# Recurrence of a hybrid layer: 32-blocks of the inverse paired into one block-diagonal product, and the value weights split inside the last turn

## The reference, cut to what matters

```python
def _rwkv7_scan(r, w, k, v, a, b):
    def step(state, inp):
        r_t, w_t, k_t, v_t, a_t, b_t = inp
        sa = jnp.einsum('bhvk,bhk->bhv', state, a_t)
        state = (state * w_t[:, :, None, :] + sa[..., None] * b_t[:, :, None, :]
                 + v_t[..., None] * k_t[:, :, None, :])
        return state, jnp.einsum('bhvk,bhk->bhv', state, r_t)
```

## Time and profile before

| what | value |
|---|---|
| median of three runs | 1833.14 us |
| the profiled execution, its time | 1833.6 us |
| its span, first to last instruction | 1831.8 us |
| stretch of the 8 turns of the recurrence | 223.2 to 503.8 us |
| TensorE busy in the whole span | 93% |
| TensorE busy in that stretch | 233 of 280.5 us |
| mean granted clock of TensorE, whole span and stretch | 0.96 and 0.87 of full |

### The profile page before, as it was taken

The page is one execution under the profiler, slowest core; times in us unless marked ns, Lnnn a source line. Parts: engine busy times, 40 slices in busy tenths (PEclk is TensorE's granted clock), DMA queues, the critical chain, the costliest instruction groups (busy, mean ns, idle before and its releaser), DMA issues. The chain is left out here.

```text
span 1831.8 us, 35801 instructions
## 1 busy us (share of the span) xinstructions
PE 1696.0 (93%) x15658; PEld 888.1 (48%) x15658; DVE 788.4 (43%) x1044; ACT 560.0 (31%) x873; POOL 454.4 (25%) x236
## 2 busy tenths in 40 slices
PE   5999678888889999889999999899999999999997
PEld 2444366766644455544444444444444444444443
DVE  5766555567422455611310168632323232332328
ACT  5212253455322455631221226431203021221210
POOL 1221122112021111212333302362325141423220
PEclk9999787899889999999999999999999999999999
DMA  9463000000102020041212031222111120202002
GB/s 356 145 195 126 12 4 4 4 4 4 50 24 70 24 58 1 1 138 35 57 46 57 0 115 35 92 93 69 35 59 47 49 84 19 81 24 92 0 1 92
DMA packets 105700, 109.94 MB, mean 60 GB/s; under 512 B 2508, under 2 KB 82522, under 8 KB 105306
## 3 DMA queue, kind: packets, MB, share of 16 engines
q1 hardware_dynamic: 105560, 107.82, 18.3%
HBM read 101.52 MB, written 4.19 MB: 58 GB/s over the span
## 5 line engine op out<-in xcount | busy, mean ns | idle before, releaser
L208 PE MATMUL tokens_ps<-a_hi,z 128*128 128x512 bf16 x960 | 248.9, 381 | 2.9 <-ACT ff_r L2167 2.8
L591 PE MATMUL ff_ps<-ff_hi,c_hi 128*128 128x512 bf16 x512 | 194.0, 379 | 0.9 <-DVE z L2271 0.9
L591 PE MATMUL ff_ps<-ff_lo,c_hi 128*128 128x512 bf16 x512 | 194.0, 379 | 0.0
L591 PE MATMUL ff_ps<-ff_hi,c_lo 128*128 128x512 bf16 x512 | 194.0, 379 | 0.0
L2271 DVE TENSOR_TENSOR z<-ff_ps,z 128x512 f32<-128x512 f32 x128 | 88.3, 690 | 204.6 <-PE ff_ps L591 204.2
L2167 ACT ACTIVATE ff_r<-tokens_ps,cols 128x1024 f32<-128x1024 f32 x32 | 35.6, 1114 | 436.6 <-PE tokens_ps L208 427.4
L208 PEld LDWEIGHTS tokens_ps<-a_hi,z 128*128 128x128 bf16 x960 | 94.0, 98 | 117.3 <-issue 5.3
L2094 POOL TENSOR_TENSOR z<-z 128x1024 bf16<-128x1024 f32 x28 | 62.2, 2221 | 352.8 <-ACT z L2090 352.8
L208 PE MATMUL tokens_ps<-a_lo,z 128*128 128x512 bf16 x480 | 143.2, 380 | 0.0
L2259 DVE TENSOR_TENSOR ff_r<-ff_r 128x1024 f32<-128x1024 f32 x32 | 41.1, 1285 | 226.9 <-ACT ff_r L2167 226.7
L185 POOL TENSOR_TENSOR mg_wlo<-mg_stage,mg_whi 128x1024 bf16<-128x1024 f32 x21 | 45.7, 2177 | 158.0 <-ACT mg_whi L181 158.0
(11 more groups left out here) (352 smaller groups left out, 3162.9 us busy)
## 6 DMA issues: line engine op xcount, KB each, us to landing
ada_w<-w_ada SPq DMA_DIRECT2D x8, 2048.0 KB, 8.1
ff_st<-w_ff SPq DMA_DIRECT2D x8, 2048.0 KB, 7.8
z<-w_ff SPq DMA_DIRECT2D x30, 512.0 KB, 4.1
mg_stage<-w_in SPq DMA_DIRECT2D x16, 512.0 KB, 4.1
zs_stage<-w_in SPq DMA_DIRECT2D x14, 512.0 KB, 6.9
z<-w_ada SPq DMA_DIRECT2D x6, 1024.0 KB, 13.5
z<-w_in SPq DMA_DIRECT2D x8, 512.0 KB, 4.9
z<-w_out SPq DMA_DIRECT2D x1, 4096.0 KB, 14.3
```

The source lines that it names most:

```text
L208: last = pe.matmul(out[:, h * HALF:(h + 1) * HALF], w[:, kt, :], a[:, slot, h * HALF:(h + 1) * HALF], start=(x == 0 and y == 0), stop=(x = ...
L591: last = pe.matmul(out, a[:, slot, at], w[:, x, n], start=(x == 0 and y == 0), stop=(x == k - 1 and y == 2))
```

## The change

Four edits in the recurrence:

1. The two 32-blocks of a chunk become one 64x64 block-diagonal matrix. `X` and `NTm` become 64 wide (masks of the levels with zeros outside the two diagonal blocks), and `correction` and `corrected` loop over 2 row groups of 64 instead of 4 of 32: 16 products, with 64x64 weights and 32 moving columns.
2. `X` must be block-diagonal, so ScalarE's copy becomes two copies, each scaled by a column of zeros and ones (`misc(5)`, `misc(6)`), each on half of the columns.
3. The roles of `Ts` and `TTs` are exchanged: the sum goes to `TTs` (semaphore `TTe`) and the transpose to `Ts` (semaphore `Te`, four more counts), because `X` is now the weights of `corrected`. The `correction` of the next step waits for `Te`.
4. The 8 `value_weight` of the last turn are no longer behind the scaling of `PQ` but spread over the turn: behind `vn`, correction 2, `kn`, correction 3, `centred`, `T12e`, `squared` and `answers`. `rhs` now shares the buffer of `PQ`, with a wait for `HY` of the turn before ahead of `an`.

The constants `misc` move into the free columns of `small`, and the tile `levels` becomes two. GpSimd's list and SyncE's are unchanged.

The diff, cut to its core (left out: the other uses of `misc` and unchanged lines):

```diff
...
@@ -55,18 +56,20 @@
     t[:, CT["small"]] = np.select([which == 0, which == 1], [upper(1), row == col], 0)
-    t[:, CT["levels"]] = np.select([which == k for k in range(4)], [upper(2 << k) for k in range(4)])
+    own = i % CH // 32 == j % CH // 32
+    for k in range(4):
+        t[:, CT["levels"] + k // 2] += np.where(own & (j // CH == k % 2), upper(2 << k), 0)
     t[:, CT["bones"]] = i // HD == j // HD
...
@@ -896,14 +899,15 @@
                   for at in (PAIRS, PAIRS + 2)] for c in (g.c_hi, g.c_lo))
-        NTd, NTm = sb("NTd", (P, NB, CH)), sb("NTm", (P, NB, 3, B))
-        X, TTs, Ts, T64 = sb("X", (P, NB, B)), sb("TT", (P, NB, B)), sb("T", (P, NB, B)), sb("T64", (P, NB, CH))
-        rhs, PQ = sb("rhs", (P, NB, P)), sb("PQ", (P, NB, P))
+        NTd, NTm = sb("NTd", (P, NB, CH)), sb("NTm", (P, NB, 3, CH))
+        X, TTs, Ts, T64 = sb("X", (P, NB, CH)), sb("TT", (P, NB, B)), sb("T", (P, NB, B)), sb("T64", (P, NB, CH))
+        PQ = sb("PQ", (P, NB, P))
+        rhs = PQ
         gt, st = sb("gt", (P, NC, HD)), sb("st", (P, NC + 1, HD))
...
         BAB, BCD, HY = (BA, BB), (BC, BD), (HY0, HY1)
-        per_turn = {"M1e": 2, "NTd": 2, "NTm": 2, "PQa": NT, "M2e": 2, "TTm": 2, "T12e": 2, "ze": 2, "ge": 2, "ysb": 2, "PQ": 2, "TTe": 4, "Te": 5, "X": 4, "Xe": 4, "TX": 4,
+        per_turn = {"M1e": 2, "NTd": 2, "NTm": 2, "PQa": NT, "M2e": 2, "TTm": 2, "T12e": 2, "ze": 2, "ge": 2, "ysb": 2, "PQ": 2, "TTe": 4, "Te": 5, "X": 4, "Xe": 8, "TX": 4,
                     "ch": NC, "S": NC}
@@ -1021,7 +1025,9 @@
                 wait(act, t, "X", k + 1)
-                act.activation(flat(X[:]), BD[:, 0:2 * P], ACT.Copy).then_inc(s["Xe"], 1)
+                for h in range(2):
+                    act.activation(X[:, :, h * B:(h + 1) * B], BD[:, 0:2 * P].rearrange("p (b n) -> p b n", n=B), ACT.Copy,
+                                   scale=g.misc(5 + h)).then_inc(s["Xe"], 1)
 
@@ -1072,10 +1078,17 @@
                     act.wait_ge(s["vw"], 16)
+                    wait(act, TURNS - 1, "k2")
                 act.activation(v_hi[:, kt, :], v_stage[:, kt, :], ACT.Copy).then_inc(s["vhi"], 1)
...
                 f, n, l, ll, lll = t % 2, t + 1, t - 1, t - 2, t - 3
+
+                def values_ahead(*kts):
+                    if t == TURNS - 1:
+                        for kt in kts:
+                            value_weight(kt)
+
                 state_maps(l)
@@ -1084,30 +1097,36 @@
                 natural(t, "vn", flat(vn[:]), BA[:])
+                values_ahead(0)
                 correction(t, 2)
+                values_ahead(1)
                 decays(n)
                 natural(t, "kn", flat(kn[:]), BB[:])
+                values_ahead(2)
                 correction(t, 3)
+                values_ahead(3)
                 natural(t, "bn", W[f][:, :, 1, :].rearrange("p (e j) n -> p j e n", e=2), q4(BA).rearrange("p j (e n) -> p j e n", e=2))
+                wait(act, l, "HY")
                 natural(t, "an", rhs[:, :, 0:HD].rearrange("p (e j) n -> p j e n", e=2), q4(BB).rearrange("p j (e n) -> p j e n", e=2))
...
                 centred(ll)
+                values_ahead(4)
                 wait(act, t, "T12")
...
                 act.activation(T64[0:B, :, B:CH], BC[0:B, 0:2 * P].rearrange("p (b n) -> p b n", n=B), ACT.Copy).then_inc(s["T12e"], 1)
+                values_ahead(5)
                 wait(act, t, "mv")
...
                 squared(ll)
+                values_ahead(6)
                 high(lll)
                 answers(l)
+                values_ahead(7)
                 wait(act, t, "PQ", 2)
...
                     act.activation(PQ[:, 4 + j, :], BB[:, j * P:(j + 1) * P], ACT.Copy, scale=rn[t % 2][:, 2 * j + 1:2 * j + 2]).then_inc(s["PQa"], 1)
-                if t == TURNS - 1:
-                    for kt in range(KT):
-                        value_weight(kt)
 
@@ -1151,8 +1170,8 @@
             eye = small(1)
-            level = lambda k: g.tile("levels")[:, k * B:(k + 1) * B]
-            upper_levels = g.tile("levels")[:, B:4 * B].rearrange("p (k n) -> p k n", n=B).unsqueeze(1).to_broadcast([P, NB, 3, B])
+            levels = g.const[:, CT["levels"]:CT["levels"] + 2, :].rearrange("p a (k n) -> p (a k) n", n=CH)
+            upper_levels = levels[:, 1:4, :].unsqueeze(1).to_broadcast([P, NB, 3, CH])
             strict, incl = (g.tile("causal")[:, x * CH:(x + 1) * CH] for x in range(2))
@@ -1283,10 +1302,11 @@
                 wait(dve, t, "TX", k + 1)
-                wait(dve, t, "Te", k + 1)
-                dve.tensor_tensor(flat(Ts[:]), BD[:, 2 * P:4 * P], flat(Ts[:]), ALU.add).then_inc(s["Te"], 1)
-                wait(dve, t, "Te", k + 2)
-                dve.transpose(flat(TTs[:]), flat(Ts[:])).then_inc(s["TTe"], 1)
+                if k:
+                    wait(dve, t, "TTe", k)
+                dve.tensor_tensor(flat(TTs[:]), BD[:, 2 * P:4 * P], flat(TTs[:]), ALU.add).then_inc(s["TTe"], 1)
+                wait(dve, t, "TTe", k + 1)
+                dve.transpose(flat(Ts[:]), flat(TTs[:])).then_inc(s["Te"], 1)
 
@@ -1306,9 +1326,9 @@
                 dve.transpose(flat(Ts[:]), flat(TTs[:])).then_inc(s["Te"], 1)
-                dve.tensor_tensor(X[:], NTd[:, :, 0:B], over(level(0), NB), ALU.mult).then_inc(s["NTm"], 1)
+                dve.tensor_tensor(X[:], NTd[:], over(levels[:, 0, :], NB), ALU.mult).then_inc(s["NTm"], 1)
                 queries(l, 1)
-                dve.tensor_tensor(NTm[:], NTd[:, :, 0:B].unsqueeze(2).to_broadcast([P, NB, 3, B]), upper_levels, ALU.mult).then_inc(s["NTm"], 1)
+                dve.tensor_tensor(NTm[:], NTd[:].unsqueeze(2).to_broadcast([P, NB, 3, CH]), upper_levels, ALU.mult).then_inc(s["NTm"], 1)
                 queries(l, 0)
@@ -1338,7 +1358,7 @@
                 wait(dve, t, "X21")
-                dve.tensor_copy(flat(X[:]), BD[:, 0:2 * P]).then_inc(s["X21e"], 1)
+                dve.tensor_copy(X[:, :, 0:B], BD[:, 0:2 * P].rearrange("p (b n) -> p b n", n=B)).then_inc(s["X21e"], 1)
                 state(l, 7)
...
@@ -1536,17 +1556,17 @@
                 for e, j, b in blocks:
-                    for q in quads:
-                        last = pe.matmul(BD[q, b * B:(b + 1) * B], NTm[q, b, k - 1, :] if k else X[q, b, :], Ts[q, b, :], start=True, stop=True)
+                    for rows in rows2:
+                        last = pe.matmul(BD[rows, b * B:(b + 1) * B], NTm[rows, b, k - 1, :] if k else X[rows, b, :], Ts[rows, b, :], start=True, stop=True)
                 last.then_inc(s["X"], 1)
...
             def corrected(t, k):
-                wait(pe, t, "Xe", k + 1)
+                wait(pe, t, "Xe", 2 * k + 2)
                 if k:
...
                 for e, j, b in blocks:
-                    for q in quads:
-                        last = pe.matmul(BD[q, (NB + b) * B:(NB + b + 1) * B], TTs[q, b, :], X[q, b, :], start=True, stop=True)
+                    for rows in rows2:
+                        last = pe.matmul(BD[rows, (NB + b) * B:(NB + b + 1) * B], X[rows, b, :], TTs[rows, b, :], start=True, stop=True)
                 last.then_inc(s["TX"], 1)
@@ -1635,7 +1655,7 @@
                     for q in (1, 3):
-                        last = pe.matmul(BC[quads[q - 1], b * B:(b + 1) * B], X[quads[q], b, :], TTs[quads[q], b, :], start=True, stop=True)
+                        last = pe.matmul(BC[quads[q - 1], b * B:(b + 1) * B], X[quads[q], b, 0:B], TTs[quads[q], b, :], start=True, stop=True)
                 last.then_inc(s["T12"], 1)
...
```

More of the change, by code:

```diff
@@ L43 @@
 PAIR_ROWS = ("w0", "a0", "kk", "ka", "rk", "gng", "gnb")
-CT = {n: i for i, n in enumerate(("ident", "causal", "small", "levels", "bones", "cent", "ahead", "misc"))}
+CT = {n: i for i, n in enumerate(("ident", "causal", "small", "levels", "levels2", "bones", "cent", "ahead"))}
+MISC = 64
 def constants():
@@ L61, in constants @@
     t[:, CT["ahead"]] = j >= i
[L62 to L69, removed]
+    t[:, CT["small"], MISC + 0] = i[:, 0] < HD
+    t[:, CT["small"], MISC + 1] = i[:, 0] >= HD
+    t[:, CT["small"], MISC + 2] = ADALN_EPS
+    t[:, CT["small"], MISC + 3] = LN_EPS
+    t[:, CT["small"], MISC + 4] = GN_EPS
+    t[:, CT["small"], MISC + 5] = i[:, 0] % CH < CH // 2
+    t[:, CT["small"], MISC + 6] = i[:, 0] % CH >= CH // 2
+    t[:, CT["small"], MISC + 7] = i[:, 0] % 32 == 0
     reset = np.ones((P, HALF), np.float32)
@@ L1409, in squares @@
                 for j in range(NT):
-                    last = pe.matmul(F[:, 2 * j:2 * j + 2], tmp[:, j * P:(j + 1) * P], g.const[:, CT["misc"], 0:2], start=True, stop=True)
+                    last = pe.matmul(F[:, 2 * j:2 * j + 2], tmp[:, j * P:(j + 1) * P], g.const[:, CT["small"], MISC:MISC + 2], start=True, stop=True)
                 last.then_inc(s["ss"], 1)
@@ L1458, in variance @@
                 for j in range(NT):
-                    last = pe.matmul(TL[:, 2 * j:2 * j + 2], ysb[l % 2][:, j * P:(j + 1) * P], g.const[:, CT["misc"], 0:2], start=True, stop=True)
```

(3 more changed lines are left out.)

## The result

The changed kernel takes 1851.07 us (median of 15 runs, 1831.69 to 1861.03) against 1834.38 (15 runs, 1829.26 to 1844.98) before: ratio 1.007, 95% interval 1.0046 to 1.0093. That is slower by 0.7%, where I forecast 1825 and faster; 1851 is also outside the range of 1811 to 1841.

The account below looks back on a forecast made before the run. TensorE bounds the kernel, held up by instruction-queue gaps and a lowered clock. Turns 1 to 6 -6.9, turn 0 +3, turn 7 -2.5, value split -1.4: -7.8 from 1833.6 is 1825.8, as median 1825; range 1811 to 1841.

Parts of the forecast that it names:

- What bounds the kernel, and the gaps: Turns: TensorE bounds; instruction-queue gaps of 4.0 us a turn mostly go, packets 64 to about 48, "issue" waits under 12 us.
- fifth rival: Turns: the gaps are not the instruction queue and stay, +26 us, 1851; chance 0.10.
- Wider products: `correction` and `corrected` groups: 0.95 + 0.16 = 1.11 us each for 0.84, +2.2 us a turn over eight groups.
- second rival: 64x64 groups: the weight load is hidden, 0.78 us a group instead of 1.11, -14 us, 1811; chance 0.10.
- Copies, transpose, masks: Each step: two copies 0.89 us (+0.51), sum and transpose 0.91 (+0.49), wider `NTm` up to 0.95 more.
- The turn at the full clock: One turn against turn 5: 33.6 - 4.15 + 2.2 + 1.95 - 0.6 = 33.0 us.
- pipelines that fill twice: Groups broken by gaps: each fills its pipeline twice, 0.2 us for each of 3.75 gaps a turn, saved when gaps go.
- The value split: Last turn and behind: GpSimd's cuts still take 8.96 us; only the 1.93 ahead of them goes, less 0.5: -1.4 us.
- Clock: Turns 1 to 6: lower-level time falls from 8.7 to 5.5 us a turn at 0.35 each, costing 1.9 a turn.
- third rival: Turns: the clock stays as it is, +8 us, 1833, no change; mean clock under 0.87 would show it; chance 0.20.
- Turn 0: First turn, with little cover: four longer steps cost 6.2 us, less some 2 of gaps and 1.2 of cover: +3.
- Turn 7: Last turn, 35.1 us before: gains its gaps and part of its lower clock, with less cover: -2.5 us.

Follow-up runs that it names:

- first product alone: Changed kernel without the value split, `corrected` back to 32x32, one copy, transpose off the way, only `correction` 64x64: 1806.03 us, ratio 0.9844 to the kernel before.
- second in 32: Changed kernel without the value split, `corrected` back to 32x32 products, two copies and transpose on the way kept: 1825.03 us, ratio 0.9952 to the kernel before.
- both wide, short chain: Changed kernel without the value split, one copy, corrections 1 to 3 taking the sum untransposed: 1821.37 us, ratio 0.9941 to the kernel before.
- double columns: Changed kernel without the value split, each 64x64 product streaming its 32 moving columns twice, blocks reordered for that: 1814.94 us, ratio 0.9917 to the kernel before.
- order control: Changed kernel without the value split, blocks reordered as for doubled columns but with 32 moving columns: 1848.43 us, ratio 1.0111 to the kernel before.

## Why the prediction was wrong, point by point

*What bounds the kernel, and the gaps: right.* 48 packets, 10.7 us of "issue" waits for the 12 that I set as the bound. My fifth rival, with gaps that stay, is refuted; that its 1851 is also the measured time is chance. The bursts of the earlier trace rows lie 4.4, 3.6 and 3.6 us apart, so my "no less than about 3.8" was their mean and not their least. The sentence of the Trainium skill ("Runtime: NRT & Kernel Launch", Instruction fetch mechanics) that I cited, that block crossings are mostly hidden, isn't borne out here: with 16 packets fewer, 21 us of waits went away, and with 8 fewer (first product alone) 16.7.

*Wider products: right.* From start to start they take 1.01 and 1.05 us, where I had 0.95 ahead of the change of shape on the other side. On that side a chain piece, which needs 0.12, takes 0.16 to the start of `corrected` (433.07 to 433.23) and 0.33, its wait left out, to that of `correction` (434.82 to 435.31, less 0.16). Together that is 1.05 and 1.26 for my 1.11. For the old group I had misread this side in the row that I cited: 0.34 less 0.12 is 0.22 and not 0.16, so that group cost 0.90 and not 0.84, and the difference stays near my +0.27. The second rival (0.78) is refuted, and with it the idea that the new group is faster.

*Copies, transpose, masks: right.* Turn 5 on ScalarE and on VectorE:

```profile
436.48 0.84 ACT L1029 ACTIVATE rec_X<-rw_invx,const 128x256 f32<-128x256 f32 x2 [0.96 <-PE rw_invx L1560]
```

```profile
425.47 1.74 DVE L1331 TENSOR_TENSOR rec_NTm<-rec_NTd,const 128x1536 f32<-128x1536 f32 x1
...
434.35 0.42 DVE L1307 TENSOR_TENSOR rec_TT<-rw_invx,rec_TT 128x256 f32<-128x256 f32 x1
434.81 0.45 DVE L1309 STREAM_TRANSPOSE rec_T<-rec_TT 128x256 f32<-128x256 f32 x1
```

The pair of copies takes 0.84 (0.89 forecast), sum and transpose 0.91 (0.91), `NTm` 1.74 (up to 1.90).

*The turn at the full clock: right in its sum, with luck in its terms.* 32.5 us for the forecast 33.0, turn 5 before being 33.6. In turn 5 TensorE waits 0.4 us for the transpose and not at all for the copies, where I had 1.95 together (0.9 a turn over all eight). Against that stand waits that I didn't have, 0.6 for VectorE's `zt` and 0.4 more for ScalarE's `PQ`. What takes back the rest, some 0.6 us, I can't name; my 0.75 for pipelines that fill twice is the term with the least behind it.

*The value split: right in its mechanism.* GpSimd's cuts now follow `low` at once and take as long as before, 8.95 us for eight, and TensorE still waits 5.1 us for them (the last line):

```profile
526.47 1.16 POOL L970 TENSOR_TENSOR c_lo<-rec_yc,c_hi 128x512 bf16<-128x512 f32 x1 [33.13 <-ACT c_hi L1076]
527.58 8.95 POOL L980 TENSOR_TENSOR z<-z 128x512 bf16<-128x512 f32 x8
```

```profile
PE rw_tail L1436 <- POOL z L980: 5.1, 1, 5.1
```

-1.5 for the forecast -1.4 in that wait. In the time of the whole no run shows it clear of the noise.

***Clock*: the step that failed.** I put the us at the lower level at 5.5 a turn for 8.7, because the gaps lay ahead of those stretches. In the profiled executions the eight turns have 70.7 us there before and 128.8 after, 16.1 a turn. The price was about right (0.35 against a fitted 0.40); the amount moved the wrong way. With the measured amounts my own sum nearly closes: turns 1 to 6 have 91.7 us at the lower level for my 33, turn 0 has 37.1 for the 12.7 that I left as they were, and 0.35 x 83.1 is 29 us on the 1825.8 of the forecast, 1854.9; the profiled execution took 1855.9.

So the step that failed is the sentence that, with the gaps, some of the stretches at the lower level go. What my sum put at nothing is that the rest of the change can bring such stretches. One part of the change seems to have two effects on the clock. It takes away gaps, and L falls (first product alone: by 42 us). And it replaces 64 pairs in 0.68 us by 32 pairs in 1.01 to 1.05, whose pace doubled columns don't change, so that TensorE streams half the columns in more time while the busy row looks fuller than before. I had worked out that the weight load sets the group's pace, and used this only for its duration. The second product has few gaps left to remove (1.3 us of waits with the long chain, 5.2 with the short one) and pays the whole price. The longer chain, which I priced by its open waits alone, is the other half of the loss: without it both wide products together took 1821, less than before (with other numbers in them). My third rival named the right place (the clock and not the gaps decides), but let it only stay as it was, 1833; its condition, a mean clock in the turns below 0.87, was met (0.79 over all eight).

*Turn 0:* +11.3 us for the forecast +3; its 40.5 us are at 0.54, 37.1 us of them at the lower level for 12.7 before. At the price of 0.4 that is +9.8 of it. Part of this is the scatter of single executions: the old turn 0 took 29.2 us in one profile and 34.9 in another, while all profiled kernels with both products wide and single columns have it at 0.50 to 0.56. *Turn 7:* 33.9 for 35.1, -1.2 for -2.5.

**Shown and open.** Shown: the loss goes with the clock (the runs' own line). It needs both the second wide product (second in 32: 1825) and the long chain (both wide, short chain: 1821, with other numbers in the products), and it is undone by streaming more columns in the same time (double columns against its control). Shown too: the long chain costs nothing measurable with 32x32 products and 19 to 26 us beside wide ones. Only argued is why these combine as they do: that short waits and groups that stream little together cost TensorE its clock. The first product alone seems to have that price too, hidden behind what its gaps give back: with double columns its L is 70 for 91, both with the value split. Not tried were double columns in the 32x32 groups of the kernel before, which would tell whether the columns matter there too, and both products wide with double columns and the short chain.

## What to carry to other kernels

Don't read a full busy row of TensorE as a promise of its clock. Here groups of small products that wait on their weight loads looked busy, and the clock was lower than with twice the columns in the same groups. Ahead of a change that makes weights larger or moving operands narrower, price what happens if the clock falls, and read the granted clock by stretch in the profile after, from more than one execution. When a change has two parts that each repeat, time each alone before judging the whole: here half of it is worth 29 us and the rest costs more than that. And where a group keeps its length with more moving columns, as here, it is cheap to try whether useless ones pay.

## What the runs showed of the hardware

- TensorE was busy for 82% of a stretch of 42 us by the trace (34.4 of 42.0) and stayed at 1.2 GHz through all of it (granted clock 0.50, order control, turn 0). With double columns the same turn was busy for 72% (22.7 of 31.6) at a granted clock of 0.86.
- 32 pairs of 64x64 float32 weights on two tile places took nearly the same time with 32 and with 64 moving columns, 1.05 and 1.07 us; at the lower level the 32-column group took 1.85. 64 pairs of 32x32 took 0.68.
- The "issue" waits of the turns went with the packets of the instruction queue: 32.0 us with 64, 15.3 with 56 (first product alone), 10.7 with 48.
- Between executions of one program the time at the lower level differed by a factor of 1.5 (132 to 201 us of the changed kernel), and the time of the run with it, by 0.3 to 0.4 us for each us. For this kernel few runs tell little (15 and 15 gave the ratio to within 0.24%), and a line of time against the clock says more than the medians.
